# Where the adaptive-modulation products of a 14-stage transformer kernel run, and what fills TensorE's waits at stage changes

## The chip, the cores and the metric

The kernel runs on one core of one Trainium2 chip. The metric is device time in microseconds (us) for one execution; lower is better. TensorE (PE in the profile) multiplies matrices, VectorE (DVE) and ScalarE (ACT) work element by element, SyncE (SP) and ScalarE issue the DMAs, GpSimd (POOL) does next to nothing here. TensorE's clock has two levels, 1.2 and 2.4 GHz; the profile gives the granted clock as a share of 2.4 GHz, so 0.50 is 1.2 GHz and 1.00 is 2.4 GHz.

## The reference, cut to what matters

Four transformer layers are computed on 256 tokens of width 1024 in fp32. Two belong to a first model (gated feed-forward with hidden width 2816), two to a second (squared ReLU, hidden width 4096), whose first layer mixes tokens by pooling and also runs on a second stream of context tokens. Every layer is adaptively modulated. In the reference, for layer `i`:

```python
mod = jax.nn.silu(c) @ ada_w[i] + ada_b[i]
sh_a, sc_a, g_a, sh_f, sc_f, g_f = jnp.split(mod[:, None, :], 6, axis=-1)
h = rms_norm(x, attn_norm[i]) * (1.0 + sc_a) + sh_a
...
x = x + g_a * y
h = rms_norm(x, ffn_norm[i]) * (1.0 + sc_f) + sh_f
x = x + g_f * swiglu(h, ffn_w_gate[i], ffn_w_up[i], ffn_w_down[i])
```

So each layer needs six modulation vectors of 1024 numbers (a shift, a scale and a gate for the mixer and for the feed-forward part): 24 vectors in all, each the product of one row with a 1024 x 1024 matrix of 4 MB. They depend on the condition `c` alone and not on the tokens, so they may be computed at any time before they are used.

## The kernel before, in words

**Stages.** The kernel is one hand-ordered program per engine. The stages are: three input products (`in0_2`, `in0_0`, `in0_1`), attention 0, its output product `out0`, `up0` and `down0` (feed-forward), `in1_0` to `in1_2`, attention 1, `out1`, `up1`, `down1`, then for each of two streams a pooling product, `up2x` and `down2x`, then `kvc`, `q3`, `kvl`, attention 3, `out3`, `up3`, `down3`. Weights come in units of 1 MB through four raw buffers (`wraw`), on SyncE's queue. For each unit ACT rounds to a high part (`whi`, L569) and DVE subtracts to get the low part (`wlo`, L956); TensorE then makes several products of high and low parts (L1604 to L1606 in row and down stages, L1667 and L1668 in up stages). In an up stage DVE adds up the two halves of each unit's result (L978), which marks the pace of that stage.

**A stage change.** When a panel of results is done, DVE multiplies it by the gate and adds it to the residual `res` in four quarters (L1042, L1044), ACT squares each quarter (L659), DVE gets the inverse root (L1050 to L1056) and scales the rows (L1073), TensorE transposes them (L1732; in the two pooling stages it multiplies by the pooling matrices, L1729), and ACT and DVE apply scale and shift (L672, L1090) and split the result `hT` in two. Only then can the next stage's products start. In between TensorE also spreads a gate vector over all partitions (`gate()`, L1752) once the residual has emptied the banks that it uses.

**Modulation units.** Each of the 24 vectors is made by four units (`vector_unit`, L1576): a unit waits for its 1 MB of `ada_w` and multiplies it into PSUM bank 7. After the fourth, DVE adds the result to the bias in `modrow` (`vector_out`, L919). `columns` transposes three rows into columns (L1593), which DVE copies (L935, L939). The 96 units are numbered r = 4g + j. Units 2 to 7 are loaded early into `work`; all the others go through `ring`, which has two slots, in turn. ACT issues these loads on its own queue (`ring_dma`, L340), in program order with its other work: a load first waits until the unit that had its slot is used (`ring_used`).

**Order by hand.** `STEP_PLAN` lists the vectors whose units run one by one at `ada_step` calls: 0 and 1 at the start, 2 to 4 in the `in0` products, 5 in `out0`, 9 and 10 in attention 1 (one unit for each step), 11 in `out1`, 21 and 22 in attention 3, 23 in `out3`. `STREAM_PLAN` places the rest behind weight units: 12 units (vectors 6 to 8) in `up0`, 20 (12 to 16) in `up1`, 4 (17) in `down1`, 12 (18 to 20) in `up21`. In attention a step of TensorE is `scores`, `turn` and `values` (L1814 or L1802, L1829, L1848 or L1841), then the unit. No units run between the end of one stage and the first product of the next. `columns(1, 1)` runs after attention 1 and `columns(2, 1)` after `down1`; on DVE both stand ahead of what follows there (the normalisation of the attention rows, L1463 to L1468, and the residual).

Of the kernel before, what the change touches and what calls it, by code (L numbers as in the profile page):

```python
# [11 lines left out]
ALU = mybir.AluOpType  # L12
# [79 lines left out]
def build(nc, x, c, positions, ada_w, ada_b, attn_norm, ffn_norm, ffn_w_gate, ffn_w_up, ffn_w_down,  # L92
# [6 lines left out]
    with stack:  # L99
# [74 lines left out]
        LINK_BANK = 7  # L174
        xn = wk(12288, 2048).rearrange("p (t n) -> p t n", t=TT)
# [140 lines left out]
        STEP_PLAN = [0, 1, 2, 3, 4, 5, 9, 10, 11, 21, 22, 23]  # L316
        STREAM_PLAN = {"up0": (6, 3), "up1": (12, 5), "down1": (17, 1), "up21": (18, 3)}
# [5 lines left out]

        def ring_view(r):
            return wk((r - EARLY.start) * 2048, 2048) if r in EARLY else ring[:, r % 2, :]

        def ring_dma(eng, r):
# [12 lines left out]
            eng.dma_start(dst, src).then_inc(early_full[r] if r in EARLY else ring_full[r % 2], 16)  # L340

        def ring_wait(eng, r):

            if r in EARLY:
                eng.wait_ge(early_full[r], 16)
                return
            landed = 16 * (r // 2 + 1 - (len(EARLY) // 2 if r >= EARLY.stop else 0))
            eng.wait_ge(ring_full[r % 2], landed)
# [49 lines left out]
        def att(stage):  # L398
# [9 lines left out]
            a.ada = {0: 0, 1: 8, 3: 8}[stage]  # L408
# [114 lines left out]
        def _(act):  # L523
# [19 lines left out]
            def ada_step(n=1):  # L543

                for _ in range(n):
                    q, j = step_no[0] // 4, step_no[0] % 4
                    step_no[0] += 1
                    if q < len(STEP_PLAN):
                        ring_fill(ring_at(STEP_PLAN[q], j) + 3)
# [44 lines left out]
            def stream(name, hold_last=False):  # L594
# [4 lines left out]
                first, many = STREAM_PLAN.get(name, (0, 0))  # L599
                for i in range(s_["count"]):  # L600
# [6 lines left out]
                    if i < 4 * many:  # L607
                        ring_fill(ring_at(first + i // 4, i % 4) + 3)
# [219 lines left out]
            for n in range(3):  # L828
                row_segment(f"in1_{n}", heads=(1, n - 1) if n else None)
# [9 lines left out]
            row_segment("out1", ada=True)  # L839
# [8 lines left out]
            for s_ in range(2):  # L848
# [1203 lines left out]
```

## Time and profile before

| what | value |
|---|---|
| median of 3 runs | 1703.57 us (1698.58 to 1705.34) |
| the profiled execution, time | 1700.29 us |
| its span, first to last instruction | 1698.5 us |
| mean granted clock | 0.944 |
| busy: TensorE, DVE, ACT | 1533.6, 1044.4, 724.0 us |
| DMA | 336 MB, mean 198 GB/s |
| chain that ended last, by engine | PE 66%, DVE 21%, ACT 6%, issue 3%, DMA 3% |

A matmul's end is modelled, so neighbours overlap in the records: the distance of their starts is the pace. The chain that ended last follows, from the last instruction back, what released each step; an engine's share of it is time that the result really waited for.

### The profile page before, as it was taken

What the parts mean: (1) busy time and instruction counts of PE and PEld (TensorE: products, weight loads), DVE (VectorE), ACT (ScalarE), POOL (GpSimd) and SP (SyncE); (2) the same over time, 40 slices, a digit from 0 to 9 for tenths busy, and PEclk for the clock granted to TensorE, in tenths of its full rate; (3) what the DMA queues carried; (4) which work ended last, traced back from release to release, by engine and by line L of the source; (5) the groups of instructions that cost most, each with busy time, mean ns of one, the idle gap of its engine ahead of it and who ended that gap; (6) DMA issues with size and microseconds to landing.
All of it is one profiled execution on the core that took longest, in us unless ns stands there. A gap on an engine that the chain in (4) does not pass through costs nothing.

```text
span 1698.5 us, 21648 instructions
## 1 busy us (share of the span) xinstructions
PE 1533.6 (90%) x8849; PEld 1224.5 (72%) x8849; DVE 1044.4 (61%) x1701; ACT 724.0 (43%) x1098; POOL 0.2 (0%) x4
## 2 busy tenths in 40 slices
PE   3997889999988789999979999799998886999997
PEld 1776767788776557777758878677886764778786
DVE  2584546566669856556576555765556686366555
ACT  1343524334444424334435554344544443345543
POOL 0000000000000000000000000000000000000000
PEclk9997889999998989999979999999999898989999
DMA  9972156865544656887734555468654343545552
GB/s 354 360 269 100 51 174 233 306 230 174 198 142 156 224 173 224 302 312 281 242 115 149 185 187 188 147 218 302 223 184 164 126 172 124 174 125 176 182 187 87
DMA packets 165835, 336.25 MB, mean 198 GB/s; under 512 B 8160, under 2 KB 109160, under 8 KB 165480
## 3 DMA queue, kind: packets, MB, share of 16 engines
q1 hardware_dynamic: 138880, 230.90, 40.4%
q10 hardware_dynamic: 26856, 103.96, 16.9%
q8 instruction: 70, 1.15, 0.3%
q14 instruction: 29, 0.24, 0.0%
HBM read 333.79 MB, written 1.05 MB: 197 GB/s over the span
## 4 chain that ended last, share of the span: by engine, by line
PE 66%; DVE 21%; ACT 6%; issue 3%; DMA 3%; ACTq 0%; SPq 0%; DVEq 0%
PE ps L1667 13%; PE ps L1604 11%; PE ps L1605 11%; PE ps L1606 11%; DVE wlo L956 7%; PE ps L1668 6%; PE ps L1576 4%; ACT whi L569 3%; DVE hbuf L978 2%; PE ps L1732 2%; DVE res L1044 1%; DMA ring<-in_ada_w_dram 1%; DVE work L1042 1%; ACT hbuf L589 1%; PE ps L1729 1%
## 5 line engine op out<-in xcount | busy, mean ns | idle before, releaser
L956 DVE TENSOR_TENSOR wlo<-wraw,whi 128x1024 fp32r<-128x1024 f32 (+1 forms) x424 | 498.1, 1216 | 321.1 <-ACT whi L569 320.7
L569 ACT ACTIVATE whi<-wraw 128x1024 fp32r<-128x1024 f32 (+1 forms) x424 | 422.6, 1044 | 311.8 <-PE ps L1606 155.3
L1667 PE MATMUL ps<-hT,whi 128*128 128x512 f32 x1472 | 529.2, 403 | 0.0
L1668 PE MATMUL ps<-hT,wlo 128*128 128x256 f32 x1472 | 413.5, 281 | 0.0
L1667 PEld LDWEIGHTS ps<-hT,whi 128*128 128x128 f32 x1472 | 278.3, 189 | 85.3 <-issue 18.1
L1668 PEld LDWEIGHTS ps<-hT,wlo 128*128 128x128 f32 x1472 | 279.4, 190 | 0.0
L1604 PE MATMUL ps<-whi,act_hi 128*128 128x512 f32 x560 | 219.4, 392 | 4.1 <-DVE wlo L956 3.9
L1605 PE MATMUL ps<-wlo,act_hi 128*128 128x512 f32 x560 | 218.1, 390 | 0.0
L1606 PE MATMUL ps<-whi,act_lo 128*128 128x512 f32 x560 | 217.9, 389 | 0.0
L1604 PE MATMUL ps<-whi,hT 128*128 128x512 f32 (+2 forms) x416 | 163.1, 392 | 6.4 <-DVE hT L1093 6.4
L1605 PE MATMUL ps<-wlo,hT 128*128 128x512 f32 (+2 forms) x416 | 159.2, 383 | 0.0
L1606 PE MATMUL ps<-whi,hT 128*128 128x512 f32 (+2 forms) x416 | 158.5, 381 | 0.0
L950 DVE TENSOR_TENSOR act_lo<-work,act_hi 128x512 fp32r<-128x512 f32 x70 | 48.4, 692 | 170.4 <-ACT whi L569 170.3
L1604 PEld LDWEIGHTS ps<-whi,act_hi 128*128 128x128 f32 x560 | 105.1, 188 | 30.8 <-DVE wlo L956 6.3
L565 ACT ACTIVATE act_hi<-work 128x512 fp32r<-128x512 f32 x70 | 44.1, 630 | 181.2 <-issue 170.9
L1606 PEld LDWEIGHTS ps<-whi,act_lo 128*128 128x128 f32 x560 | 105.1, 188 | 22.1
L1605 PEld LDWEIGHTS ps<-wlo,act_hi 128*128 128x128 f32 x560 | 105.1, 188 | 21.6
L1604 PEld LDWEIGHTS ps<-whi,hT 128*128 128x128 f32 x416 | 79.8, 192 | 32.0 <-issue 9.1
L1576 PE MATMUL ps<-ring,cpad 128*32 128x256 f32 x1440 | 97.6, 390 | 3.4 <-DMA ring<-in_ada_w_dram 2.8
L1606 PEld LDWEIGHTS ps<-whi,hT 128*128 128x128 f32 x416 | 79.4, 191 | 15.3
L1605 PEld LDWEIGHTS ps<-wlo,hT 128*128 128x128 f32 x416 | 79.6, 191 | 14.0
L978 DVE TENSOR_REDUCE hbuf<-ps 128x512 f32<-128x1024 f32 x70 | 85.1, 1218 | 2.1 <-PE ps L1668 2.1
(198 smaller groups left out, 1260.7 us busy)
## 6 DMA issues: line engine op xcount, KB each, us to landing
wraw<-in_mlp_w_dram SPq DMA_DIRECT2D x96, 1024.0 KB, 5.2
ring<-in_ada_w_dram ACTq DMA_DIRECT2D x90, 1024.0 KB, 6.8
wraw<-in_ffn_w_gate_dram SPq DMA_DIRECT2D x22, 1024.0 KB, 5.4
wraw<-in_ffn_w_up_dram SPq DMA_DIRECT2D x22, 1024.0 KB, 7.1
wraw<-in_ffn_w_down_dram SPq DMA_DIRECT2D x22, 1024.0 KB, 4.9
wraw<-in_diff_w_in_dram SPq DMA_DIRECT2D x12, 1024.0 KB, 5.0
wraw<-in_attn_w_qkv_dram SPq DMA_DIRECT2D x12, 1024.0 KB, 5.0
wraw<-in_sp_w_in_dram SPq DMA_DIRECT2D x8, 1024.0 KB, 13.3
```

The source lines that it names most:

```text
L565: nc.scalar.activation(act_hi[:, u % 2, :], hid[:, at:at + 512], ACT.Copy)
L569: nc.scalar.activation(whi[:, u % 2, part], raw_view(u)[:, part], ACT.Copy).then_inc(hi_ready, 1)
L950: nc.vector.tensor_tensor(act_lo[:, u % 2, :], hid[:, at:at + 512], act_hi[:, u % 2, :].bitcast(F32), ALU.subtract)
L956: nc.vector.tensor_tensor(wlo[:, u % 2, part], raw_view(u)[:, part], whi[:, u % 2, part].bitcast(F32), ALU.subtract).then_inc(lo_ready, 1)
L978: nc.vector.tensor_reduce(dst.rearrange("p (f n) -> p f n", f=2), hidden_banks(i), AX, ALU.add).then_inc(hid_sum, 1)
L1576: ins = mm(ps[32 * c_:32 * c_ + 32, ADA_BANK, 0:256], cpad[:, 0 if g < 12 else 1, kt, :], ring_view(r)[:, kk * D + 256 * c_:kk * D + 256 * ...
L1604: mm(dst, s_hi, m_hi, start=start, stop=False, skip_group_check=skip)
L1605: mm(dst, s_hi, m_lo, start=False, stop=False, skip_group_check=skip)
L1606: return mm(dst, s_lo, m_hi, start=False, stop=stop, skip_group_check=skip)
L1667: mm(ps[:, bank, :], whi[:, u % 2, c0:c0 + P], hT[:, :, k, :], start=(k == 0), stop=False, skip_group_check=True)
L1668: ins = mm(ps[:, bank, 0:S], wlo[:, u % 2, c0:c0 + P], hT_hi[:, k, :], start=False, stop=(k == KT - 1), skip_group_check=True)
L1732: ins = nc.tensor.transpose(ps[:, T_BANKS[n][b], (k % 2) * S + t * P:(k % 2) * S + (t + 1) * P], xn[:, t, k * P:(k + 1) * P], ident)
```

## The change

It moves modulation units out of the streams and attention 3 into the places between two stages, adds two more slots (`("x", 0)` and `("x", 1)`) at columns 8192 and 10240 of `work` for the third and fourth unit of eight vectors, adds products of constants whose results nobody reads (`idle_products`), moves two `columns` calls, splits the last bias load into twelve, and makes one DVE reduction in attention 1 wait for its own end.

```diff
+        IDLE_BANK = 0
+        IDLE_NORM = {1: 7, 2: 6, 4: 2, 8: 6, 9: 2, 10: 5}
+        IDLE_GATE = {1: 5, 2: 6, 4: 4, 9: 6}
+        IDLE_HEADS = {1: 5, 3: 46}
+        IDLE_ROWS = 4
...
-        STEP_PLAN = [0, 1, 2, 3, 4, 5, 9, 10, 11, 21, 22, 23]
-        STREAM_PLAN = {"up0": (6, 3), "up1": (12, 5), "down1": (17, 1), "up21": (18, 3)}
+        STEP_PLAN = [(g, j) for g in range(6) for j in range(4)] + [(9, 2), (9, 3)] + [(10, j) for j in range(4)] + [(11, 0), (11, 1)]
+        STREAM_PLAN = {"up0": (6, 2, 0), "up1": (13, 3, 2), "down1": (16, 1, 0)}
+        BESIDE_FILL = {"down0": (2, 36), "down1": (5, 72), "up20": (2, 80), "up21": (2, 88), "up1": (0, 54)}
+        FOUR_SLOTS = (8, 12, 17, 18, 19, 20, 21, 22)
...
+            slot = ("early", r) if r in EARLY else ("x", j - 2) if g in FOUR_SLOTS and j >= 2 else ("ring", r % 2)
...
-            if r >= EARLY.stop:
-                before = r - 1 - (len(EARLY) if r < EARLY.stop + 2 else 0)
-                eng.wait_ge(ring_used, before)
+            if slot_before[r] >= 0:
+                eng.wait_ge(ring_used, slot_before[r] + 1)
...
-            a.ada = {0: 0, 1: 8, 3: 8}[stage]
+            a.ada = {0: 0, 1: 8, 3: 0}[stage]
```

On ACT (the loads; `ring_fill(n)` issues all loads below unit n that are not yet issued):

```diff
+            def bias_last(slots):
+                for strm in range(2):
+                    for v in slots:
+                        act.dma_start(modrow[strm:P:32, v, :], adab[3][:, v * D:(v + 1) * D].rearrange("a (j n) -> (a j) n", j=4)).then_inc(bias_landed, 16)
...
+                row_segment(f"in1_{n}", ..., beside=(lambda i: ring_fill(38) if i == 1 else None) if n == 0 else None)
...
+            def next_vector(i):
+                if i == 1:
+                    act.wait_ge(ATT[1].taken, ATT[1].steps)
+                    ring_fill(52)
+            row_segment("out1", beside=next_vector)
...
                 if s_ == 0:
                     held_split("down1")
+                    ring_fill(76)
+                    bias_last((0, 1, 3, 4))
                 else:
                     held_split("down20")
+                    ring_fill(84)
...
+            row_segment("kvc", beside=lambda i: ring_fill(92) if i == 1 else None)
...
+                row_segment(name, heads=(3, n), beside=(lambda i: ring_fill(94) if i == 1 else None) if n == 0 else None)
...
+            ring_fill(96)
             gate()
             turns(3)
```

On DVE, the reduction in attention 1 (`vector_out` and `columns` move with their units):

```diff
-                        nc.vector.tensor_reduce(stat[:, TT * i:TT * i + TT], o2, AX, ALU.add)
+                        link(nc.vector.tensor_reduce(stat[:, TT * i:TT * i + TT], o2, AX, ALU.add))
...
             attention(1)
-            columns(1, 1)
...
-            stream("down1", hold_last=True)
-            columns(2, 1)
+            stream("down1", hold_last=True, beside=lambda i: columns(2, 1) if i == 6 else None)
```

On TensorE:

```diff
+            def idle_products(bank, many):
+                for _ in range(many):
+                    mm(ps[:, bank, :], half_r[:, 0:P], causal_r[:, :, :, :].rearrange("p h b n -> p (h b n)"), start=True, stop=True, skip_group_check=True)
...
             down_segment("down0")
+            vector_units(8, 0, 4)
             norm()
             for n in range(3):
                 row_segment(f"in1_{n}")
+            vector_units(9, 0, 2)
             gate()
+            idle_products(IDLE_BANK, IDLE_HEADS[1])
             pe.wait_ge(sem("heads1"), 1)
             turns(1)
             turned(1)
             attention(1)
-            columns(1, 1, 11)
+            vector_units(11, 2, 4)
             out_turn(1)
-            row_segment("out1", ada=True)
+            row_segment("out1", beside=lambda i: columns(1, 1, 12) if i == 2 else None)
+            vector_units(12, 0, 2)
             gate()
+            vector_units(12, 2, 4)
             norm()
             up_segment("up1")
...
             for strm in range(2):
+                pooled_vector, hidden_vector = (17, 18) if strm == 0 else (19, 20)
+                vector_units(pooled_vector, 0, 4 if strm == 0 else 3)
                 gate()
+                vector_units(pooled_vector, 4 if strm == 0 else 3, 4)
                 norm()
...
+                vector_units(hidden_vector, 0, 3)
                 gate()
+                vector_units(hidden_vector, 3, 4)
                 norm()
...
+            vector_units(21, 0, 4)
             norm()
             row_segment("kvc")
+            vector_units(22, 0, 4)
             norm()
             row_segment("q3")
             row_segment("kvl")
+            vector_units(23, 0, 2)
             gate()
+            vector_units(23, 2, 4)
+            idle_products(IDLE_BANK, IDLE_HEADS[3])
             pe.wait_ge(sem("heads3"), 1)
             turns(3)
...
-            row_segment("out3", ada=True)
+            row_segment("out3")
```

`norm()`, `gate()` and `out_turn(1)` begin with the `idle_products` that `IDLE_NORM`, `IDLE_GATE` and `IDLE_ROWS` give for their number.

## Rows read from the trace of the kernel before

**Rows 1.** The page: busy time by engine, and TensorE's granted clock in 40 slices.
```profile
PE 1533.6 (90%) x8849; PEld 1224.5 (72%) x8849; DVE 1044.4 (61%) x1701; ACT 724.0 (43%) x1098; POOL 0.2 (0%) x4
...
PEclk9997889999998989999979999999999898989999
```
**Rows 2.** Timeline of DVE in the first `up` stream: start us, duration us.
```profile
348.13 1.22 DVE L978 TENSOR_REDUCE work<-ps 128x512 f32<-128x1024 f32 x1
354.98 1.22 DVE L978 TENSOR_REDUCE hbuf<-ps 128x512 f32<-128x1024 f32 x1
360.64 1.22 DVE L978 TENSOR_REDUCE work<-ps 128x512 f32<-128x1024 f32 x1
```
**Rows 3.** The same view in `up20`, which has no modulation units, and in `up21`.
```profile
909.69 1.22 DVE L978 TENSOR_REDUCE hbuf<-ps 128x512 f32<-128x1024 f32 x1
915.50 1.22 DVE L978 TENSOR_REDUCE hbuf<-ps 128x512 f32<-128x1024 f32 x1
...
1153.88 1.22 DVE L978 TENSOR_REDUCE hbuf<-ps 128x512 f32<-128x1024 f32 x1
1160.73 1.22 DVE L978 TENSOR_REDUCE hbuf<-ps 128x512 f32<-128x1024 f32 x1
```
**Rows 4.** Timeline of TensorE in the last attention: one step, one unit, the next step.
```profile
1438.22 1.98 PE L1802 MATMUL ps<-work 128*128 128x512 f32 x4
...
1442.80 1.07 PE L1576 MATMUL ps<-ring,cpad 128*32 128x256 f32 x16
1443.80 1.98 PE L1802 MATMUL ps<-work 128*128 128x512 f32 x4
```
**Rows 5.** Waits of TensorE: who waited for whom, us in total, times, longest us.
```profile
PE ps L1732 <- DVE work L1073: 42.9, 9, 14.0
...
PE ps L1771 <- DVE mark L1520: 17.4, 1, 17.4
```
**Rows 6.** Windows at the change after `down1`: PE, PEld, DVE, ACT, POOL, PEclk, DMA, GB/s.
```profile
850.00:857.00 7.00, 7.00 (x34) 5.75 (x32) 2.91 (x3) 2.01 (x2) 0.00 (x0) 1.00 0.57 173
857.00:861.00 4.00, 0.21 (x2) 0.00 (x0) 3.62 (x11) 1.00 (x3) 0.00 (x0) 0.97 1.08 387
861.00:871.00 10.00, 7.02 (x16) 4.30 (x17) 7.33 (x24) 1.89 (x6) 0.00 (x0) 0.50 0.22 92
```
**Rows 7.** Timeline: 16 transposes after a wait, and 16 straight after attention.
```profile
258.18 3.68 PE L1732 MATMUL ps<-cst,work 128*128 128x128 f32 x16 [2.42 <-DVE work L1073]
...
1467.84 1.91 PE L1874 MATMUL ps<-cst,work 128*128 128x128 f32 x16
```
**Rows 8.** Windows, columns as in rows 6, while TensorE runs the turns of attention 1.
```profile
549.00:552.00 3.00, 1.86 (x9) 1.87 (x10) 2.62 (x7) 1.78 (x4) 0.00 (x0) 0.50 0.00 0
552.00:555.00 3.00, 3.00 (x23) 3.00 (x21) 1.99 (x4) 1.20 (x2) 0.00 (x0) 0.74 0.41 111
```
**Rows 9.** Timeline at the ends of `down0` and `down1`: last product, residual's DVE instructions.
```profile
463.49 0.39 PE L1606 MATMUL ps<-whi,act_lo 128*128 128x512 f32 x1
...
466.61 0.69 DVE L1044 TENSOR_TENSOR res<-res,work 128x512 f32<-128x512 f32 x1
...
856.38 0.39 PE L1606 MATMUL ps<-whi,act_lo 128*128 128x512 f32 x1
...
862.65 0.69 DVE L1044 TENSOR_TENSOR res<-res,work 128x512 f32<-128x512 f32 x1
```
**Rows 10.** The chain that ended last: two transfers that something waited for.
```profile
558.82 5.37 DMA ring<-in_ada_w_dram
...
1075.76 7.39 DMA work<-in_pool_scale_dram
```
**Rows 11.** Timeline after the first pool product: ACT's split, the gate, the transposes.
```profile
877.86 1.99 ACT L569 ACTIVATE whi<-wraw 128x1024 fp32r<-128x1024 f32 x2
...
886.13 3.78 PE L1752 MATMUL ps<-modrow,cst 32*128 32x256 f32 x8 [3.54 <-DVE work L1042]
...
890.76 2.61 PE L1732 MATMUL ps<-cst,work 128*128 128x128 f32 x11 [0.86 <-DVE work L1073]
```

More of the change, by code:

```diff
@@ L598, in stream @@
                     act.wait_ge(hid_done, hid_base[name[4:]] + s_["count"])
-                first, many = STREAM_PLAN.get(name, (0, 0))
+                first, many, off = STREAM_PLAN.get(name, (0, 0, 0))
+                fill_at, fill_to = BESIDE_FILL.get(name, (-1, 0))
                 for i in range(s_["count"]):
@@ L606, in stream @@
                         split_unit(s_["base"] + i + 2)
[L607 to L608 removed]
+                    if 0 <= i - off < 4 * many:
+                        ring_fill(ring_at(first, i - off) + 3)
+                    if i == fill_at:
+                        ring_fill(fill_to)
             def square_heads(layer, n):
@@ L982, in hidden_out, with stream @@
                     nc.vector.tensor_tensor(dst, dst, hbuf[:, n % 2, :], ALU.mult).then_inc(hid_done, 1)
-            def stream(name, hold_last=False):
+            def stream(name, hold_last=False, beside=None):
                 s_ = by_name[name]
-                first, many = STREAM_PLAN.get(name, (0, 0))
+                first, many, off = STREAM_PLAN.get(name, (0, 0, 0))
                 for i in range(s_["count"]):
@@ L992, in stream @@
                         split_unit(s_["base"] + i + 2)
-                    if i < 4 * many and i % 4 == 3:
-                        vector_out(first + i // 4)
+                    if 0 <= i - off < 4 * many and (i - off) % 4 == 3:
+                        vector_out(first + (i - off) // 4)
+                    if beside is not None:
+                        beside(i)
             def row_segment(name, hold_last=True, ada=False, heads=None, own=False):
@@ L1471, in _, with second_norm @@
             out_turn(1)
-            row_segment("out1", ada=True)
+            def second_norm(i):
+                if i == 0:
+                    vector_out(11)
+                if i == 2:
+                    columns(1, 1)
+            row_segment("out1", heads=second_norm)
             residual(0)
@@ L1495, in _ @@
             held_split("down21")
-            row_segment("kvc")
+            row_segment("kvc", heads=lambda i: vector_out(21) if i == 0 else None)
             panel_rows(kvc, 0, 1024)
@@ L1620, in emptied, with vector_units, row_segment @@
                     pe.wait_ge(dve_emptied, dve_count[n])
-            def row_segment(name, ada=False):
+            def vector_units(g, first, last):
+                for j in range(first, last):
+                    vector_unit(g, j)
+            def row_segment(name, ada=False, beside=None):
                 s_ = by_name[name]
@@ L2018, in _ @@
             attention(3)
-            columns(3, 1, 23)
+            columns(3, 1, 24)
             out_turn(3)
-            row_segment("out3", ada=True)
+            row_segment("out3")
             gate()
```

93 lines of the change are left out of this document (56 added, 37 removed).

## The prediction

> **What bounds the kernel now.** I read the page first. TensorE is busy for 90% of the span, DVE for 61%, and the granted clock falls in slices spread over the whole run [rows 1]. So two things are to be looked for: work on TensorE that could leave its path, and what happens where the clock falls. The pace of the streams is seen in the spacing of DVE's L978, one for each weight unit. In `up0` it is 6.85 us in the first part (1153.88 to 1160.73 in `up21` is the same) and 5.66 us once the modulation units have ended [rows 2, 3]. In `up20`, without any, it is 5.81 us [rows 3]. TensorE sets that pace: a weight unit with a modulation unit behind it costs 1.19 us more in the gated streams and 1.04 us more in the others. In attention 3 a step is 5.58 us and holds a unit of 1.07 us, and the next step's product starts as the unit ends [rows 4]. Third the waits: TensorE waits 42.9 us in nine norms for L1073 and 17.4 us once before the turns of attention 3 [rows 5]. Last the windows at one change: TensorE works 7.00 of 7 us before it, 0.21 of 4 us in it, and for the following 10 us the clock is 0.50 [rows 6]. So a stage change costs twice: the wait, and the slow transposes and first products behind it. Sixteen transposes take 3.68 us there, against 1.91 us where TensorE comes straight from attention [rows 7].
>
> **Part 1, units leave the streams.** I count 40 units placed between stages: 4 each after `down0`, `out1`, `down1`, both pooling products, `down20`, `down21`, `kvc` and `kvl`, 2 before the gate that leads to attention 1, 2 after attention 1. Out go 4 from `up0` and 8 from `up1` at 1.19 us (14.3 us) and 12 from `up21` at 1.04 us (12.5 us) [rows 2, 3]; 4 from `out1`, 4 from `out3` and 8 from attention 3 at 1.07 us (17.1 us) [rows 4]. Attention 1 keeps its number, `down1` too. Sum 44 us off TensorE's path. In attention 3 the next limit is the chain scores, maximum, exponential, turn; a unit of 1.07 us out of 5.58 us leaves TensorE the limit, I think, so I take the full price; the other end is nothing of its 8.6 us.
>
> **Part 2, the same units in the waits.** After a down stage the last residual instruction ends 3.8 us after the last product starts (463.49 to 467.30), and normalisation and scaling follow [rows 9]; TensorE idles some 8 us. Four units at 1.07 us end inside that and start at the full clock, as they follow at once. Where the four loads were issued a stage earlier (after `down0`, `out1`, `down1`, `down20`, `down21`) I take nothing for them; what hides them is DVE's residual and norm, and if that cover were gone they would cost 4.3 us a change. After `kvc` the wait is short and 4 MB are asked for during a 22 us product, so 1 us is taken (0 to 4).
>
> **Part 3, loads that come late.** Here the change pays back. After each pooling product the four units (vectors 18 and 20) are loaded only by the `ring_fill` behind ACT's held split, at 877.86 in the first stream [rows 11]. A transfer of 1 MB takes 5.37 us to land when alone [rows 10], and at the 387 GB/s of a full window [rows 6] each further MB takes 2.7 us. So the four land at about 883, 886, 889 and 891, some 2.7 us later with the weight unit that goes at the same time. Three stand ahead of the gate (3.78 us, at 886.13) and the fourth ahead of the transposes, at 890.76 (the gate's end 889.9) [rows 11]. TensorE takes its instructions in order, so gate and transposes queue behind the loads: third unit at 891 to 892, gate, fourth unit, transposes at about 896. I take 5 us for each of the two places (0 to 8). ACT also issues eight small bias loads there, some 3 us, which end before it is needed.
>
> In attention 1 units 36 and 37 used to lie ready, and unit 38, asked for at 558.82, landed 5.37 us later, when two steps of scores were out [rows 10]. Now 36 and 37 are used ahead of the gate, and 38 is asked for only behind the first step's exponentials, yet stands behind the first scores. The second scores wait for the load, and the next units come in pairs at one latency each. By the pacing of the steps the third step begins some 6.5 us later; I take 6.5 (0 to 8).
>
> **Part 4, the clock.** Ten changes get work that follows closely enough: after `out0`, `down0`, `in1_2`, attention 1, `out1`, `down1`, `down20`, `down21`, `kvc`, `out3`. The transposes shrink by 1.8 us [rows 7], of which some 1.3 us reaches the next product, since DVE and ACT work through the first group meanwhile; the first products at half clock add 0.5 us on average. 1.8 us for each, 18 us. Bounds: nothing if the clock falls all the same, 25 us if all of both comes back. No trace shows the constant products; with 512 columns like a weight product I price them at about 0.23 us, 0.43 us at half clock, and they lie inside the waits. The exception is the 46 before attention 3: units 94 and 95 wait for a load until about 1403, and 46 products then take 10 to 12 us, so that they end as the 17.4 us wait ends [rows 5] or up to 3 us later; the turns get faster by about as much. Nothing is taken.
>
> The trace and the notes differ on transposes. Through 549 to 555 us TensorE runs the transposes L1771, and the granted clock goes from 0.50 to 0.74 on the way [rows 8]; it rose on transposes. The Trainium skill, page "TensorE: Matmul & The Clock Gate", section "Part 4: PE-mode transpose", says that the full clock does not engage for transposes, which do not count as busy in the same way. By that rule the clock would fall again during the 16 transposes, and the first products would be slow as before.
>
> **Part 5, small moves.** `columns(2, 1)` leaves the head of the residual after `down1`: there the residual ended 7.0 us after the last product started (856.38 to 863.34), after `down0` 3.8 us [rows 9]. 3 us are gained; the pooling constants, asked for at the stage's end and 7.39 us on the way [rows 10], are late next. Three `vector_out` in front of a residual or turn, the linked reduction of attention 1 and the moved `columns(1, 1)` net to 2 us lost.
>
> **Sum.** 44 + 18 + 3 = 65 gained; 10 + 6.5 + 1 + 2 = 19.5 lost; net 45.5. The profiled execution took 1700.29 us, so 1654.8; the median of the runs is 3.3 us above it, so 1658.
>
> **Rivals.** *The loads are in time.* If the pooling loads land before the gate's slot and attention 1 hides its first, 16.5 us come back: 1642. For it: the DMA queues are empty then. Against: the order of ACT's instructions. 0.13.
>
> *The clock is not held.* The fills end several us before the transposes, and the clock falls in that rest: 18 us less, 1676. For it: after `down1` it fell within a wait of 4 to 5 us [rows 6]. Against: 4 units leave less than that. 0.18.
>
> *Transposes end the full clock.* The clock falls while they run, the first products are slow, and half of the 18 us goes: 1667. Against it stands [rows 8]. The page named above states this rule. 0.04.
>
> *The streams don't get faster* because splits or weight loads take over from TensorE, so that the change doesn't do what it says: 27 us of part 1 stay, 1685. Against it: 5.66 us in `up0` without units [rows 2]. 0.06.
>
> *Slower than before.* At all eleven changes with units TensorE is stuck in order behind loads not yet landed, as the transfers of weights and units share the queues. It loses the 45.5 us at 4.1 us a change more than I took, and passes 0.5% (8.5 us) at 4.9 us, about the latency of one load [rows 10]. With a full latency (5.37 us) at each, 1717. Against it: six of the eleven are asked for a stage ahead. 0.04.
>
> **The numbers.** My forecast, 1658, has 0.50; the last 0.05 is for mixed outcomes near no change. The range is 1634 (all loads in time, the clock's full 25 us) to 1685 (no clock, and late loads at their upper ends or streams that don't speed up). A measurement tells about 0.5% from no change: faster 0.91, same 0.05, slower 0.04.
>
> **What would show it.** L978 at 5.66 us for the second half of `up0`'s old unit range and 5.81 us throughout `up21`; steps of 4.5 us in attention 3; granted clock above 0.9 in the ten changes, and transposes of 1.9 us; L1576 waiting for its DMA after both pooling products and at the start of attention 1. It would be wrong if the clock is 0.50 at the transposes as before, or if L1576 waits for DMA at changes other than these.

## The result, and the profile after

Four executions of each kernel gave a median of 1704.38 us before and 1682.08 us after (1678.50 to 1685.13). The ratio is 0.9884, with an interval of 0.9863 to 0.9905: 22 us gained, 1.2%. The forecast was 1658. The time lies inside the range and on the side that was given, but the gain is less than half of what was foretold. The profiled execution after took 1678.50 us, its span 1676.7.

The page of the kernel after, busy time and granted clock, to be read beside [rows 1]:

```profile
PE 1552.3 (93%) x8953; PEld 1236.7 (74%) x8953; DVE 1043.2 (62%) x1701; ACT 721.4 (43%) x1098; POOL 0.2 (0%) x4
PEclk9997789999999899999989999989999998999999
```

TensorE is busy for 19 us more in a span that is 22 us shorter: the constant products (L1799, 104 of them) are busy for 32.5 us, all else for 14 us less. Line numbers have moved: a modulation unit is L1628 (L1576 before), the transposes L1792 (L1732), the gate L1818 (L1752), the reductions of the `up` streams L1019 (L978), the residual L1085 and L1087 (L1042, L1044).

TensorE's waits after, columns as in [rows 5]:

```profile
PE ps L1792 <- DVE work L1116: 17.7, 3, 12.9
PE ps L1628 <- DMA ring<-in_ada_w_dram: 15.6, 10, 6.5
PE ps L1628 <- DMA work<-in_ada_w_dram: 10.5, 4, 3.3
```

This is the result in small. The waits for the scaled rows fell from 42.9 us in nine norms to 17.7 us in three, but the units that fill them wait 26.1 us for their own loads.

I cut both traces at the first and last TensorE record of each stage. The first stretch, up to the transposes behind `out0`, holds work that the change does not touch, and took 215.9 to 226.3 us over the fourteen traces of this study. So what follows is counted from those transposes on: 1468.45 us before, 1449.53 after, 18.9 us gained. Another 2.9 us lie in that first stretch and can't be put down to the change. A "change" is the time from the last product of a stage to the first of the next. In us, with two of the later kernels beside:

| | before | after | e7 | e10 |
|---|---|---|---|---|
| `up0` and `down0` | 202.38 | 196.72 | 196.78 | 196.73 |
| change after `down0` | 10.91 | 9.66 | 10.78 | 10.82 |
| attention 1 | 43.56 | 50.70 | 43.25 | 43.32 |
| `out1` | 31.36 | 26.29 | 26.31 | 26.27 |
| change after `out1` | 9.97 | 11.23 | 11.23 | 11.22 |
| `up1` and `down1` | 215.56 | 208.32 | 208.58 | 208.12 |
| change after `down1` | 10.83 | 9.12 | 9.48 | 8.08 |
| changes after the pooling products | 23.00 | 32.24 | 23.58 | 23.65 |
| `up20` and `down20` | 181.27 | 183.43 | 182.98 | 181.31 |
| `up21` and `down21` | 195.06 | 182.74 | 182.77 | 181.50 |
| change after `kvc` | 8.00 | 14.50 | 6.76 | 6.75 |
| change after `kvl`, and turns | 28.45 | 29.40 | 29.81 | 27.89 |
| attention 3 | 47.85 | 40.65 | 40.66 | 40.66 |
| `out3` | 28.73 | 24.16 | 24.15 | 24.19 |
| change after `out3` | 9.97 | 11.38 | 11.39 | 11.17 |
| rest | 421.55 | 418.99 | 417.91 | 420.29 |
| sum | 1468.45 | 1449.53 | 1426.42 | 1421.97 |

**The streams.** DVE's reductions after, in the old unit range of `up0` and in `up20`, to be read beside [rows 2, 3]:

```profile
322.79 1.22 DVE L1019 TENSOR_REDUCE hbuf<-ps 128x512 f32<-128x1024 f32 x1
328.45 1.22 DVE L1019 TENSOR_REDUCE work<-ps 128x512 f32<-128x1024 f32 x1
...
897.59 1.22 DVE L1019 TENSOR_REDUCE hbuf<-ps 128x512 f32<-128x1024 f32 x1
903.40 1.22 DVE L1019 TENSOR_REDUCE hbuf<-ps 128x512 f32<-128x1024 f32 x1
910.73 1.22 DVE L1019 TENSOR_REDUCE hbuf<-ps 128x512 f32<-128x1024 f32 x1
```

The spacing is 5.66 us where units stood, as in the free part before. The last pair is 7.33 apart, and so is one pair in `up21`: 1.5 us are lost where ACT issues the next four modulation loads together. ACT's timeline there:

```profile
905.32 0.89 ACTq L365 DMA_DIRECT2D ring<-in_ada_w_dram  x2
906.25 1.00 ACTq L365 DMA_DIRECT2D work<-in_ada_w_dram  x2
907.36 2.01 ACT L595 ACTIVATE whi<-wraw 128x1024 fp32r<-128x1024 f32 x2 [1.41 <-issue]
```

The split of the next weight unit (L595) starts 1.41 us late behind the four issues, and it waits for no transfer: its weights had landed. DVE's split and its reduction follow it, and the chain that ended last runs through all of them. One weight load beside the four took 13.9 us to land in place of 5.4, but with four raw buffers nothing waited for it.

This also shows who sets the pace of `up20`. In the kernel before its units take TensorE 5.65 us, yet the reductions are 5.81 us apart, and from 900 to 980 us the chain that ended last is 59% DVE, 30% ACT and under 1% TensorE. In `up0` (270 to 400 us) it is 89% TensorE. So [rows 2] were read rightly, but in `up20` [rows 3] the loop of splits and reductions on ACT and DVE sets the pace, 0.15 us a unit above TensorE's own. That is why a unit costs 1.04 us there and 1.19 us in the gated streams.

**After the first pooling product.** TensorE's timeline of the kernel after, then the last two entries of ACT's queue for these loads (`[1.45 <-X]`: idle before it, and what ended it), beside [rows 11]:

```profile
865.53 1.07 PE L1628 MATMUL ps<-ring,cpad 128*32 128x256 f32 x16 [0.22 <-DMA ring<-in_ada_w_dram]
868.05 1.07 PE L1628 MATMUL ps<-ring,cpad 128*32 128x256 f32 x16 [1.45 <-DMA ring<-in_ada_w_dram]
871.32 1.93 PE L1628 MATMUL ps<-work,cpad 128*32 128x256 f32 x16 [2.20 <-DMA work<-in_ada_w_dram]
873.18 3.81 PE L1818 MATMUL ps<-modrow,cst 32*128 32x256 f32 x8
876.92 1.94 PE L1628 MATMUL ps<-work,cpad 128*32 128x256 f32 x16
```

```profile
861.64 0.66 ACTq L365 DMA_DIRECT2D work<-in_ada_w_dram  x1
862.33 4.32 ACTq L580 DMA_DIRECT2D modrow<-in_ada_b_dram  x8
```

The four loads are asked for from 860.17 to 861.64, and the units follow one another at the pace of landing. The third takes 1.93 us, since the clock has fallen in the wait. The gate stands behind it, and the fourth unit and the transposes behind the gate. The chain that ended last has the third transfer in it:

```profile
547.95 5.17 DMA ring<-in_ada_w_dram
...
861.12 10.16 DMA work<-in_ada_w_dram
...
1311.51 18.37 DMA work<-in_ada_w_dram
...
1392.05 12.44 PE ps L1799 x46
```

**After `kvc`** it is the same with a dearer price: a 1 MB load asked for at 1311.51, together with three others and the weights, lands after 18.37 us. TensorE's timeline there:

```profile
1325.99 1.07 PE L1628 MATMUL ps<-work,cpad 128*32 128x256 f32 x16 [3.34 <-DMA work<-in_ada_w_dram]
1329.93 1.94 PE L1628 MATMUL ps<-work,cpad 128*32 128x256 f32 x16 [2.87 <-DMA work<-in_ada_w_dram]
```

**Attention 1.** The first scores, the late unit, the second scores:

```profile
545.45 0.51 PE L1874 MATMUL ps<-causal_r,half_r 64*128 64x256 f32 x4 [0.83 <-ACT work L727]
...
553.17 1.94 PE L1628 MATMUL ps<-ring,cpad 128*32 128x256 f32 x16 [6.54 <-DMA ring<-in_ada_w_dram]
555.04 0.79 PE L1874 MATMUL ps<-causal_r,half_r 64*128 64x256 f32 x4
```

**The clock.** Windows of the kernel after, columns as in [rows 6], at the changes after `down0` and `out3`:

```profile
462.00:464.00 2.00, 1.89 (x17) 1.65 (x17) 1.93 (x6) 0.96 (x2) 0.00 (x0) 1.00 0.00 0
464.00:468.00 4.00, 4.00 (x18) 3.31 (x19) 3.86 (x9) 3.94 (x7) 0.00 (x0) 1.00 0.02 4
...
1477.00:1485.00 8.00, 7.85 (x29) 5.49 (x29) 5.77 (x23) 2.76 (x6) 0.00 (x0) 0.57 0.01 3
```

It was held after `down0` (1.00 at the transposes). After `down21` it fell while the transposes ran (shown with e11), and it was low after `out3`, though TensorE is busy for 7.85 of 8 us there. Sixteen transposes, 3.67 or 3.68 us before, took 2.13 us after `out0`, 1.97 after `down0` and `out1`, 2.41 after `down21`, 2.65 after `kvc` and 3.03 after `out3`. At the other four of the prediction's ten places little came back or none: 5.11 us against 5.35 for the turns of attention 1, 3.81 against 4.27 for the transposes behind attention 1, 8.02 against 8.81 and 9.81 against 8.56 for the two pooling multiplications.

### The profile page after: what moved, and what is told of

The parts are those of the page before. It is cut to its first block, busy times and chain, and to the rows that moved or that the text cites. A ratio compares the mean times of both kernels' runs of the same rounds, so it can differ in the third digit from the quotient of the medians.

```text
span 1676.7 us, 21872 instructions
## 1 busy us (share of the span) xinstructions
PE 1552.3 (93%) x8953; PEld 1236.7 (74%) x8953; DVE 1043.2 (62%) x1701; ACT 721.4 (43%) x1098; POOL 0.2 (0%) x4
## 4 chain that ended last, share of the span: by engine, by line
PE 60%; DVE 22%; ACT 7%; DMA 6%; issue 3%; ACTq 1%; SPq 0%; DVEq 0%
PE ps L1655 11%; PE ps L1656 11%; PE ps L1657 11%; PE ps L1724 10%; DVE wlo L997 8%; PE ps L1725 5%; ACT whi L595 4%; PE ps L1628 3%; DVE hbuf L1019 3%; DMA work<-in_ada_w_dram 2%; DMA ring<-in_ada_w_dram 2%; ACT hbuf L615 2%; PE ps L1799 1%; PE ps L1789 1%; PE ps L1895 1%
## 5 line engine op out<-in xcount | busy, mean ns | idle before, releaser
L595 ACT ACTIVATE whi<-wraw 128x1024 fp32r<-128x1024 f32 (+1 forms) x424 | 422.5, 1044 | 281.9 <-PE ps L1657 146.6
L1657 PEld LDWEIGHTS ps<-whi,act_lo 128*128 128x128 f32 x560 | 105.5, 188 | 22.3
L1628 PE MATMUL ps<-ring,cpad 128*32 128x256 f32 x1184 | 82.4, 405 | 17.1 <-DMA ring<-in_ada_w_dram 15.6
L1019 DVE TENSOR_REDUCE hbuf<-ps 128x512 f32<-128x1024 f32 x70 | 84.9, 1217 | 0.4 <-PE ps L1725 0.4
```

The source lines that it names most:

```text
L595: nc.scalar.activation(whi[:, u % 2, part], raw_view(u)[:, part], ACT.Copy).then_inc(hi_ready, 1)
L1019: nc.vector.tensor_reduce(dst.rearrange("p (f n) -> p f n", f=2), hidden_banks(i), AX, ALU.add).then_inc(hid_sum, 1)
L1628: ins = mm(ps[32 * c_:32 * c_ + 32, ADA_BANK, 0:256], cpad[:, 0 if g < 12 else 1, kt, :], ring_view(r)[:, kk * D + 256 * c_:kk * D + 256 * ...
L1657: return mm(dst, s_lo, m_hi, start=False, stop=stop, skip_group_check=skip)
```

## The experiments

Spans are of one profiled execution each; where three rounds were run, medians and a ratio stand beside. Stage times are cut as above.

**e1: no constant products.** From the kernel after:

```diff
-        IDLE_NORM = {1: 7, 2: 6, 4: 2, 8: 6, 9: 2, 10: 5}
-        IDLE_GATE = {1: 5, 2: 6, 4: 4, 9: 6}
-        IDLE_HEADS = {1: 5, 3: 46}
-        IDLE_ROWS = 4
+        IDLE_NORM = {}
+        IDLE_GATE = {}
+        IDLE_HEADS = {1: 0, 3: 0}
+        IDLE_ROWS = 0
```

> The changed kernel without any constant product. Theory A (the constants buy about what they cost, since they themselves run at half clock or hold up the gate behind them): total within 3 us of the changed kernel, the change after out3 some 1.5 us shorter and the wait before attention 3 some 2.5 us shorter, the change after down0 up to 1.3 us longer. Rival B (the constants hold the clock and the late loads are hidden anyway): 8 to 15 us slower than the changed kernel, with the granted clock at 0.50 during the transposes after down0, down21 and out0.

Median 1687.29 us, ratio to the kernel before 0.9917 (0.9894 to 0.9941); from `out0`'s transposes on 1453.7 us against 1449.5. The stages give 4.2 us for the constants and the medians 5.2, between the two theories, but the intervals of the two ratios overlap (0.9863 to 0.9905 with them). The clock fell without them after `down21` (transposes 3.63 us), but only partly after `down0` (2.70). They also cost: without the 46 the change after `kvl` is 22.3 us, not 24.9, while the turns take 6.4, not 4.5.

**e2, e3, e4: one place's loads a stage earlier**, each from the kernel after. For attention 1 ACT issues the next loads ahead of the turns:

```diff
+            ring_fill(40)
             turns(1)
```

For the pooling products ahead of the norm's second half, instead of behind the held split; for `kvc` the same with `ring_fill(92)`:

```diff
-                norm()
+                norm_rows()
+                ring_fill(76 if s_ == 0 else 84)
+                norm_columns()
```

> Units 38 and 39 are loaded before the turns of attention 1. Theory A (the stall at the start of attention 1 is a load that ACT asks for too late): first scores to the transposes of out1 falls from 50.7 to about 44 us, total down by 6 to 7 us. Rival B (DVE sets the pace of attention 1 and the load is covered): under 2 us.

> The loads of vectors 18 and 20 are asked for between the squares and the columns of the norm ahead of the pooling product, not behind the held split. Theory A: from the end of the pooling product to the first product of up20 and up21 it takes about 11.5 us in place of 16.1, total down by 8 to 10 us. Rival B (units in the wait cost this by themselves, through the gate and the clock): 1 to 3 us in all.

> The loads of vector 22 are asked for ahead of kvc's first product, not after its second weight unit. Theory A (two queues share the DMA engines and the 4 MB land late): from kvc's last product to q3's first 14.5 us falls to 8, total down by 5 to 6.5 us. Rival B (the bandwidth is short over the whole of kvc, and weights then come late instead): the wait moves into kvc or q3, total down by under 2 us.

Attention 1 took 43.30 us, 7.4 less. The changes after the pooling products took 11.83 us each, 8.6 less for the two together. The change after `kvc` took 6.77 us, 7.7 less. The span does not show e2's gain (1675.4), because its first stretch took 9.1 us longer; e3's is 1665.0, e4's 1671.1. In e2 the first two steps of attention 1 are:

```profile
554.72 0.51 PE L1875 MATMUL ps<-causal_r,half_r 64*128 64x256 f32 x4 [0.83 <-ACT work L727]
555.83 1.07 PE L1629 MATMUL ps<-ring,cpad 128*32 128x256 f32 x16
556.83 0.51 PE L1875 MATMUL ps<-causal_r,half_r 64*128 64x256 f32 x4
```

The second scores follow the first after 2.11 us; in the kernel after it was 9.59 us (545.45 to 555.04). In e3, after the first pooling product, and in e4, after `kvc`:

```profile
866.44 1.93 PE L1628 MATMUL ps<-ring,cpad 128*32 128x256 f32 x32
868.19 1.05 PE L1628 MATMUL ps<-work,cpad 128*32 128x256 f32 x16
870.41 2.00 PE L1818 MATMUL ps<-modrow,cst 32*128 32x256 f32 x7 [1.18 <-DVE work L1085]
```

```profile
1324.89 1.93 PE L1630 MATMUL ps<-ring,cpad 128*32 128x256 f32 x32
1326.64 1.91 PE L1630 MATMUL ps<-work,cpad 128*32 128x256 f32 x32
```

In e4 all four units run back to back at full clock. In e3 the three ahead of the gate do, and the gate then waits for the residual alone; the fourth unit, behind the gate, takes 1.63 us and the transposes 3.67, since the clock has fallen again. Late loads, not the norms, set these changes.

**e5: the units of the kernel before almost emptied**, for the vectors whose units the change moves:

```diff
                 ring_wait(pe, r)
+                if g in (8, 11, 12, 16, 18, 19, 20, 21, 22, 23):
+                    mm(ps[96:128, ADA_BANK, 0:256], cpad[:, 0, 2 * j, :], ring_view(r)[:, 0:256], start=True, stop=True).then_inc(ring_used, 1)
+                    return
                 for kk in range(2):
```

> The kernel before, with 40 units (vectors 8, 11, 12, 16 and 18 to 23, those that left streams, out1, out3 and attention 3) cut to one of their eight products each; their loads, waits and places stay, their results are wrong numbers. It measures part 1 of the prediction by itself. Theory A (TensorE sets the pace and a unit costs its 1.04 to 1.19 us): 38 to 42 us off the span less what the start varies, up0 and down0 some 4.5 us, up1 and down1 some 9 us, up21 and down21 some 11.5 us, attention 3 some 7 us. Rival B (something else takes over as the limit and this is why the change brought 20 us, not 45): under 30 us.

18 us less from `out0`'s transposes on. DVE's reductions in `up0`:

```profile
326.02 1.22 DVE L978 TENSOR_REDUCE hbuf<-ps 128x512 f32<-128x1024 f32 x1
332.42 1.22 DVE L978 TENSOR_REDUCE work<-ps 128x512 f32<-128x1024 f32 x1
```

The spacing is 6.40 us: 0.45 below the 6.85 of a full unit, 0.74 above the 5.66 of none [rows 2]. So a unit with one product of eight still costs 0.74 of 1.19 us, and 40 cut units would save 40 × 0.45 = 18 us, as measured. The match is better than its parts: a cut unit saved 0.34 us in attention 3, 0.40 in `up21`, 0.42 in `up1`, 0.48 and 0.58 in `out3` and `out1`, and 0.60 in `up0`, 17.5 us in all. My first theory took the cut unit for nearly free and missed. The rival's number came out, but not its reason (that splits or weights would take over): TensorE's records follow one another without a gap around the cut unit too, and with no unit at all the pace of the gated streams goes on down to 5.66 us. So TensorE sets the pace of the gated streams, and of `up21` while units run in it.

**e6: the units in the waits almost emptied**, in the kernel after, in the same way for vectors 8, 12 and 17 to 23.

> The changed kernel, with the 36 units of vectors 8, 12 and 17 to 23 (all that run between stages but four) cut to one of eight products each; loads and waits stay, their results are wrong numbers. Theory A (the units' own work is covered, their loads are not): the changes after the pooling products and after kvc stay at 15 to 16 and 13 to 14.5 us, only the change after out1 falls by some 2 us, total down by under 8 us. Rival B (the units' own time is what the waits can't hide): each of the changes falls by 3 to 4 us, total down by 20 us or more.

1 us less. The changes that wait for loads stayed: 15.7 and 15.1 us after the pooling products, 13.8 after `kvc`, 11.4 after `out1`. So the units' own time is covered and their transfers are not. The test is a part of a test, since by e5 a cut unit still costs most of its time: the 36 cut units took some 0.45 us each less (an estimate from e5), 16 us, of which 1 us showed.

**e7: e2, e3 and e4 together.**

> The three earlier loads (attention 1, pooling products, kvc) in one kernel. Theory A (each stall is its own and they add up): 7.4 + 8.5 + 7.5 us, so some 23 us off the changed kernel, about 1658 to 1660. Rival B (they share the DMA engines, so that an earlier load delays the weights): under 15 us.

Median 1657.37 us (1654.84 to 1659.14), ratio 0.9727 (0.9710 to 0.9745). From the transposes on 23.1 us less than the kernel after, where the three parts add to 23.7. This kernel takes what was forecast, though not by the forecast's sum. Its clock shows something else. TensorE's timeline and windows after `down0`:

```profile
462.00 1.65 PE L1802 MATMUL ps<-causal_r,half_r 128*128 128x512 f32 x6
466.06 3.45 PE L1795 MATMUL ps<-cst,work 128*128 128x128 f32 x16 [2.41 <-DVE work L1119]
```

```profile
462.00:466.00 4.00, 1.65 (x10) 1.04 (x6) 2.99 (x17) 0.65 (x2) 0.00 (x0) 0.97 0.01 2
466.00:470.00 4.00, 3.94 (x19) 3.86 (x20) 3.44 (x10) 1.90 (x4) 0.00 (x0) 0.61 0.02 4
```

The kernel after, with the same instructions there and the same idle time ahead of them, ran them at the full clock:

```profile
461.91 1.97 PE L1792 MATMUL ps<-cst,work 128*128 128x128 f32 x16 [2.40 <-DVE work L1116]
```

The whole difference at that change is 10.78 against 9.66 us. Both are single executions, so no run tells whether the kernel or the execution decides.

**e8: e7 with other fills.** From e7: all of vector 12 ahead of the gate, `IDLE_NORM {1: 4, 2: 6, 8: 8}`, `IDLE_GATE {1: 5, 2: 6, 4: 4, 9: 10}`, `IDLE_HEADS {1: 9, 3: 34}`, and in `up20` and `up21` the four loads spread over weight units 2, 4, 6 and 8:

```diff
+                    if name in ("up20", "up21") and i in (2, 4, 6, 8):
+                        ring_fill((76 if name == "up20" else 84) + i // 2)
```

> As the one before, and all of vector 12 ahead of its gate, the four loads in up20 and up21 spread over four weight units, 34 constant products before attention 3 in place of 46, none behind the wait for the pooling constants, ten ahead of out3's gate and none behind it. Theory A (fills that start late, or run at half clock just ahead of the transposes, hold them up): out1 to up1 from 11.2 to about 9, kvl to turns from 24.9 to about 22.3, out3 to up3 from 11.4 to about 9.5, down1 to pooling 1 us less, up20 and up21 1.5 us less; 8 to 11 us below the one before. Rival B (the clock falls the sooner and takes it back): within 3 us of it.

Median 1659.77 us, ratio 0.9743 (0.9727 to 0.9759): no gain over e7 by the medians, though the stages of the two traces give 2.8 us (1423.6 against 1426.4). Parts of it work: `up20` is 1.7 us shorter and `up21` 1.2, the change after `kvl` is 22.36, not 25.32 us. It is given back in `out1`'s change, 12.32 us, where the unit moved ahead of the gate meets its load late,

```profile
627.62 1.07 PE L1633 MATMUL ps<-work,cpad 128*32 128x256 f32 x16 [2.35 <-DMA work<-in_ada_w_dram]
```

and in attention 1, 45.94 us against 43.25 (this kernel has nine constants ahead of the turns of attention 1; that they are the cause is not shown). I did not try the two apart.

**e9: TensorE filled up in `out3`**, in e7, with 16 constant products in place of the units taken out there (some 3.6 us):

```diff
-            row_segment("out3")
+            row_segment("out3", beside=lambda i: idle_products(IDLE_BANK, 8) if i >= 2 else None)
```

> e7_all_ahead with eight constant products ahead of each of out3's last two weight units, 16 in all or 3.6 us of TensorE's time, about what four modulation units took there before. Theory A (without the units TensorE ends the stage 1.3 us before DVE's own queue lets the residual start, so that a part of the units was covered): out3 some 3.6 us longer and the change from out3 to up3 some 1.3 us shorter, near the 10.0 us of the kernel before, 2.3 us in all. Rival B (the change is long because the products behind the gate hold up the transposes, 11.4 us either way): the whole 3.6 us show.

`out3` grew from 24.15 to 27.93 us, but the change behind it shrank from 11.39 to 8.14. Of 3.8 us on TensorE 0.5 reach the next stage. Two things did that. One is the clock: in e7 the transposes took 3.39 us, in e9 1.97. e2 and e11 have the code of the kernel after in `out3` and the change and ran these transposes at full clock too, and their change took 10.02 us. In e2:

```profile
1481.51 1.97 PE L1793 MATMUL ps<-cst,work 128*128 128x128 f32 x16 [1.07 <-DVE work L1117]
```

So 1.4 us of the 3.25 may be the clock's, which in e2 came without any filling. The other 1.9 us are DVE's: against e11, at the same clock, the filling lengthens `out3` by 3.75 us and shortens the change by 1.88. At the end of `out3`, in the kernel after:

```profile
1469.63 2.36 DVE L997 TENSOR_TENSOR wlo<-wraw,whi 128x1024 fp32r<-128x1024 f32 x2 [3.36 <-ACT whi L595]
1471.91 0.68 DVE L1085 TENSOR_TENSOR work<-ps,gate_b 128x512 f32<-128x512 f32 x1
```

The residual starts only when DVE's last weight split ends. TensorE's last product ends at 1473.6, 1.7 us behind the residual's start. Before, after `out1`, the residual started 2.9 us ahead of that end (628.33 against 631.24); after the change it is 1.5 us (620.94 against 622.44), and in `out3` it was 2.9 us (1493.67 against 1496.57) and is 1.7. Taking units from these stages lets TensorE end sooner than DVE can follow. After `out1` there is one thing more: the two units behind the gate run at half clock (3.38 us) and hold the transposes up by 1.0 us (they start 1.95 us after DVE begins to scale the rows, before the change 0.93), which eats most of what their full clock gives back.

**e10: e7 with less fill and spread loads.** `IDLE_NORM {1: 7, 2: 6, 8: 6, 10: 2}`, `IDLE_HEADS {1: 5, 3: 34}`, and the spread loads of e8.

> e7_all_ahead with 34 constant products before attention 3 in place of 46, none in the two norms where they stand behind a late wait (4 and 9), two in place of five behind out3's gate, and the loads of vectors 19 and 21 spread over four weight units of up20 and up21. Theory A: kvl to turns 2.5 to 3 us less, the change after down1 1.2 us less, up20 and up21 1.5 us less each, 6 us below e7_all_ahead. Rival B (the clock falls the earlier and takes it back): within 2 us.

Median 1652.19 us (1648.41 to 1657.58), ratio 0.9714 (0.9691 to 0.9738): the fastest median, and 4.4 us below e7 in the stage terms. The intervals of the two ratios overlap, and e11, which is e7 with more constants, has the same stage sum (1421.8), so not all of the 4.4 us need be the trimming. The spread loads are clear: `up20` is 1.7 us shorter and `up21` 1.3. Its reductions in `up20` start 5.81 us apart at the place of the stall above too (881.76, 887.57, 893.38), since ACT issues one load (0.37 us) between two splits and the splits stay 5.81 us apart. After `down1` the change is 8.08 us: the two constants are gone that stood behind the wait for the pooling constants in the kernel after,

```profile
850.09 1.22 PE L1799 MATMUL ps<-causal_r,half_r 128*128 128x512 f32 x2 [1.21 <-DMA work<-in_pool_scale_dram]
851.11 8.03 PE L1789 MATMUL ps<-work 128*128 128x256 f32 x32
```

They ran for 1 us after the data had come.

**e11: e7 with 16 constants in place of 6** after `down0` and `down21`, so that no idle time is left.

> e7_all_ahead with 16 constant products in place of 6 after down0 and after down21, which fill the wait to within half a us of the scaled rows. Theory A (a held clock is worth only what the transposes save on the way to the next product): both changes take 9.7 us, against 10.9 at half clock, and no less. Rival B (my prediction's 1.8 us): 9.1 us or less.

```profile
462.65 3.92 PE L1802 MATMUL ps<-causal_r,half_r 128*128 128x512 f32 x16
466.70 1.97 PE L1795 MATMUL ps<-cst,work 128*128 128x128 f32 x16
```

The changes took 9.65 and 9.66 us. The window over the transposes after `down21` and the products behind them, in e11 and then in the kernel after, where 2.4 us are left idle ahead of them:

```profile
1283.00:1289.00 6.00, 5.75 (x33) 4.66 (x33) 5.79 (x14) 4.45 (x8) 0.00 (x0) 1.00 1.02 408
```

```profile
1296.00:1300.00 4.00, 4.00 (x19) 3.44 (x18) 3.86 (x10) 3.41 (x7) 0.00 (x0) 0.60 0.02 4
```

Filled to the end, the clock was held both times. With the idle time it came out either way: after `down0` 9.66 us (the kernel after, e3) or 10.78 (e7); after `down21` it fell midway in the kernel after and was held in e2 and e3 (transposes 1.97 us, changes 9.66 and 9.65). There change and `kvc` together take 34.24 us before, 32.97 after, 32.99 in e10 and 32.00 in e11.

**e12: e7 without constant products.**

> e7_all_ahead without constant products. Theory A: the constants are worth 1.2 us where they hold the clock and cost about as much where they overrun: 3 to 6 us above e7_all_ahead, about 1661 to 1664, most of it in the pooling products and the changes after down0 and down21. Rival B (with the loads in time the waits are short and the clock holds without them): within 2 us.

Median 1659.99 us, ratio 0.9768 (0.9747 to 0.9789), against e7's 1657.37. By stages 1.4 us more, by medians 2.6; the two ratios' intervals just miss each other, and the ratios, each to the kernel before run beside it, are 7 us apart. So with the loads in time the constants of e7 are worth little, 1.4 us by the traces, and the size is not well known. Against e10, run beside it, e12 takes 7.8 us more by medians and 5.8 by stages, of which 3.4 are `up20` and `up21` with their grouped loads.

## Why the prediction was off

What the cut traces give for each step, next to what it said:

| step | said | measured |
|---|---|---|
| part 1: units out of streams, `out1`, `out3`, attention 3 | +44 | +42.1 |
| changes behind `out1` and `out3` | 0 | −2.7 |
| loads late: after both pooling products | −10 | −9.2 |
| loads late: attention 1 | −6.5 | −7.1 |
| loads late: after `kvc` | −1 | −6.5 |
| loads late: ahead of attention 3 | 0 | −2.6 |
| `up20` with `down20` (four loads issued together), pooling 1 | 0 | −3.4 |
| clock, columns, small moves | +19 | +8.4 |
| sum | +45.5 | +18.9 |

Of the 26.6 us that are missing, 10.6 are in the last row, 11.3 in the loads and their issue, and 4.6 in part 1 and the changes behind it.

**Part 1 was right** in size: 5.7 in `up0` (said 4.8), 7.2 in `up1` (9.5), 12.3 in `up21` (12.5), 5.1 and 4.6 in `out1` and `out3` (4.3 each), 7.2 of 8.6 in attention 3, whose step is 4.38 us in the middle where I had taken 4.5. The 5.7 holds 1.1 us of a load stall that went away, and `up1` would have given 8.5 without a wait of 1.2 us for a late unit (at 653.14). That TensorE sets the pace is shown for the gated streams and for `up21` with its units (e5). For `up20`, and for `up21` once it is empty, I said the same and it is wrong: the loop on ACT and DVE does, at 5.81 us. The 1.04 us were taken from that difference, so the size came out all the same. What I overlooked is that in `out1` and `out3` DVE is the next to end, so that 2.7 of their 9.7 us come back in the change (the residual's start in both, and e9).

**Part 2 was right for the units' own time** (e6: 1 us in all) and failed at `kvc`. I bounded that place at 0 to 4 us, arguing that 4 MB are asked for during a 22 us product. The step fails because the issue is not where the transfer ends: beside the weights a transfer took 18.37 us where I had read 5.37 for one alone [rows 10]. e4 gives back 7.7 us, more than the change had lost (8.00 us before, 6.77 in e4).

**Part 3 was right** in mechanism and size, for the pooling products (e3) and for attention 1 (e2). Its fault is what it left out. The same delay ahead of attention 3 puts the 46 constants behind the late units: they run from 1392.05 for 12.44 us and end 2.6 us after the wait would have, of which the faster turns return 1.6. I had written "10 to 12 us" and "up to 3 us later" and then taken nothing. And I priced the transfers alone and not their issue: four issues in a row keep ACT from the next weight split, and `up20` and `up21` pay 1.5 us each for it. The 1.2 us that pooling 1 took longer are not traced to a cause.

**Part 4 is the step that failed most.** I multiplied 1.8 us by ten changes. Two things are wrong with it. A held clock is worth 0.8 to 1.3 us, not 1.8. With the stage behind the change counted in, it is 75.86 against 76.68 us after `down0` (the kernel after against e7), 32.00 against 32.99 after `down21` (e11 against e10) and, after `out3`, 191.82 in e2 against 193.09 in the kernel after, with the same code there. And it was held from the first transpose to the last at two or three of the ten changes (`down0`, `out1`, nearly after `out0`), and for a part of them at three more. Added over all ten places they shrank by 8.1 us, where I had counted on ten times 1.8. The last row of the table holds still less of the clock than its 8.4 us, as the 1.6 us of the faster turns and the 1.7 us of part 5 are in it. After `out3` the gate's products follow a wait of 1.8 us and the clock is 0.57 over the next 8 us, full as they are. The constants at half clock take 2.50 us there and hold up the transposes (in e2 they take 1.43 us there and end 1.07 us before the scaled rows):

```profile
1476.82 3.16 PE L1818 MATMUL ps<-modrow,cst 32*128 32x256 f32 x8 [1.82 <-DVE work L1085]
1479.91 2.50 PE L1799 MATMUL ps<-causal_r,half_r 128*128 128x512 f32 x5
1482.21 3.03 PE L1792 MATMUL ps<-cst,work 128*128 128x128 f32 x16
```

So the rival "the clock is not held" was mostly true, together with loads later than I had taken; it alone gave 1676. Constants earned 4 to 5 us in e1 and 1.4 to 2.6 in e12 (7 by the ratios).

**Transposes and the clock.** After `down0` 16 transposes took 1.97 us at a granted clock of 1.00, and the clock stayed at 1.00 in the 4 us of transposes and products that follow. The Trainium skill, page "TensorE: Matmul & The Clock Gate", section "Part 4: PE-mode transpose", has it that the full clock does not engage for them. These rows differ from that, and they decide. After `down21` the clock did fall during the transposes, as the rival built on that rule has it (2.41 us for the 16, the first six products at half clock). But e11, with the same transposes and no idle time ahead of them, stayed at 1.00, and in e2 and e3 they took 1.97 us even with the idle time ahead. So the transposes do not end the full clock; that the idle time does when it falls is the likelier reading, on few traces.

**Part 5**: `columns(2, 1)` gave 1.7 of 3 us after `down1`, the rest being kept by the two constants behind the data; e10 shows 2.75.

**The rivals.** "Loads in time" (1642) did not happen, and e7 makes it happen: 1657, not 1642, since the clock's share and the 2.7 us behind `out1` and `out3` are missing. "The streams don't get faster" is refuted, though its 1685 lies near the result: 25.2 of its 27 us came. It has a true part, as in `up21` the splits do take over, 0.15 us a unit above TensorE. "Slower than before" had the right mechanism, TensorE in order behind loads, but at five changes (both pooling products, attention 1, `kvc`, `kvl`) and not at eleven.

## What to carry to other kernels

Work put into a wait is free only if its operands are there when the wait begins; ask for them a whole stage ahead, one at a time between the issuing engine's own pieces of work, and price a transfer by its time beside the stage's other transfers and its issue by what the issuing engine does next. Before counting what leaves one engine, look who ends the stage next: here DVE's last split took back over a quarter of two stages' gain. A faster clock is worth what the next product gains, not what the transposes gain, and here filler earned it each time only where it reached up to the next instruction; where it stood behind a wait for data it cost its own time.

## What the runs showed of the hardware

- One column-tiled product of 128x256 in place of eight cost a stream 0.74 us where all eight cost 1.19 (e5).
- The same instructions after the same 2.4 us of idle time ran at the full clock in one kernel and mostly at half clock in another (transposes 1.97 and 3.45 us).
- A 1 MB load lands after 5.2 to 5.4 us alone, 10.16 in a group of four, and 18.37 in a group of four beside weight loads.
- Issuing four such loads kept ACT for 1.9 us (905.32 to 907.26) and cost the stream 1.5 us, though its weights had landed; one load at a time (0.37 us) cost nothing (e10).
- In an up stream without units the loop of splits and reductions on ACT and DVE took 5.81 us a unit where TensorE needed 5.65.
- The unchanged first stretch of the program took 216 to 226 us, a spread of 10 us between traces, more than most effects studied here; without cutting the traces by stage, e2 would have been read as no gain.
